# Fills and output pieces ahead of each step's turn in the second attention layer of a two-block transformer kernel

## The reference, cut to what matters

```
q, kc, vc, ks, vs, kw, vw, gl = split(h @ w_in)        # q: 1024 columns, each k and v: 256
q, ks, kw = rms_norm(q), rms_norm(ks), rms_norm(kw)    # over the 64 columns of a head
Kc = rms_norm(gelu(blocks(kc) @ w1) @ w2)              # 15 compressed keys
Vc = gelu(blocks(vc) @ w1) @ w2                        # 15 compressed values
p_c = softmax(q Kc^T * scale + bias)                   # 256 x 15 for each head
p_s = softmax(q ks^T * scale + bias)                   # 256 x 256, causal; every block is selected
p_w = softmax(q kw^T * scale + bias)                   # 256 x 256, causal
o = gate0 * p_c Vc + gate1 * p_s vs + gate2 * p_w vw
x = x + g1 * (o @ w_out)
```

## Time and profile before

| | before |
|---|---|
| median of 3 timed runs | 3153.59 us |
| lowest, highest | 3146.44, 3155.75 us |
| the profiled execution's own time | 3146.74 us |
| its span, first to last instruction | 3144.9 us |
| PE busy | 3072.9 us (98%) |
| DVE, ACT busy | 2251.2 us (72%), 1635.7 us (52%) |
| mean granted TensorE clock | 0.994 |
| the 48 steps of the loop | about 1093.8 to 1266 us of the span |

### The profile page before, as it was taken

The page is one execution under the profiler, slowest core; times in us unless marked ns, Lnnn a source line. Parts: engine busy times, 40 slices in busy tenths (PEclk is TensorE's granted clock), DMA queues, the critical chain, the costliest instruction groups (busy, mean ns, idle before and its releaser), DMA issues.

```text
span 3144.9 us, 58286 instructions
## 1 busy us (share of the span) xinstructions
PE 3072.9 (98%) x19860; PEld 2734.0 (87%) x19860; DVE 2251.2 (72%) x4124; ACT 1635.7 (52%) x3082; POOL 709.2 (23%) x710
## 2 busy tenths in 40 slices
PE   6999999999999999999999999999999999999999
PEld 5789999998788876799999888779988998988897
DVE  6649988877777535699788777777756777765654
ACT  1224568864444344355888544455456545445643
POOL 0106835530000010186555100000101010010000
PEclk9999999999999998999999999999999999999999
DMA  7644555558887441355444788877855687884454
GB/s 282 239 139 166 181 164 175 168 196 266 270 262 248 147 126 37 121 183 178 147 134 139 234 268 267 261 252 263 264 211 172 233 263 265 275 275 135 146 185 149
DMA packets 178353, 635.86 MB, mean 202 GB/s; under 512 B 24073, under 2 KB 24081, under 8 KB 177841
## 3 DMA queue, kind: packets, MB, share of 16 engines
q1 hardware_dynamic: 134560, 491.48, 47.4%
q0 software_dynamic: 43648, 142.77, 13.8%
q10 hardware_dynamic: 16, 0.01, 0.0%
HBM read 630.88 MB, written 9.53 MB: 204 GB/s over the span
## 4 chain that ended last, share of the span: by engine, by line
PE 85%; DVE 7%; DMA 3%; ACT 2%; DVEq 1%; issue 1%; SPq 0%; POOL 0%; ACTq 0%
PE ps L792 21%; PE ps L603 12%; PE ps L605 11%; PE ps L604 11%; PE ps L591 7%; PE ps L774 6%; PE ps L638 2%; PE ps L1190 2%; PE ps L1189 2%; DMA arena<-ada 1%; DMA ring<-stream 1%; PE ps L987 1%; PE ps L1054 1%; PE ps L892 1%; DVE r_outT L2459 1%
## 5 line engine op out<-in xcount | busy, mean ns | idle before, releaser
L1814 DVE TENSOR_TENSOR unit_low<-ring,unit_high 128x1024 fp32r<-128x1024 f32 x480 | 638.3, 1330 | 156.2 <-ACT unit_high L1297 147.3
L1297 ACT CAST unit_high<-ring 128x1024 fp32r<-128x1024 f32 x524 | 548.2, 1046 | 223.3 <-PE ps L605 165.4
L605 PE MATMUL ps<-expert_x_high,unit_low 128*128 128x256 f32 x1952 | 551.2, 282 | 0.0
L603 PE MATMUL ps<-expert_x_high,unit_high 128*128 128x256 f32 x1536 | 442.7, 288 | 2.5 <-DVE unit_low L1814 1.4
L604 PE MATMUL ps<-expert_x_low,unit_high 128*128 128x256 f32 x1536 | 428.4, 279 | 0.0
L605 PEld LDWEIGHTS ps<-expert_x_high,unit_low 128*128 128x128 f32 x1952 | 366.8, 188 | 0.0
L792 PE MATMUL ps<-unit_low,expert_high 128*128 128x512 f32 x1016 | 324.2, 400 | 1.3 <-DVE unit_low L1814 1.2
L792 PE MATMUL ps<-unit_high,expert_low 128*128 128x512 f32 x1016 | 319.5, 395 | 0.1
L792 PE MATMUL ps<-unit_high,expert_high 128*128 128x512 f32 x1016 | 316.6, 392 | 0.0
L603 PEld LDWEIGHTS ps<-expert_x_high,unit_high 128*128 128x128 f32 x1536 | 290.5, 189 | 7.3 <-issue 2.1
L1719 ACT CAST expert_high<-arena 128x256 fp32r (+1 forms) x256 | 103.7, 406 | 357.1 <-PE ps L792 357.1
(11 more groups left out here) (383 smaller groups left out, 7036.2 us busy)
## 6 DMA issues: line engine op xcount, KB each, us to landing
ring<-stream SPq DMA_DIRECT2D x754, 512.0 KB, 3.9
arena<-stream SPq DMA_DIRECT2D x160, 512.0 KB, 4.4
score<-ada POOLq DMA_DIRECT2D x128, 512.0 KB, 5.2
arena<-ada POOLq DMA_DIRECT2D x96, 512.0 KB, 5.3
arena<-bias_tiles POOLq DMA_DIRECT2D x48, 192.0 KB, 2.7
arena<-ada SPq DMA_DIRECT2D x8, 1024.0 KB, 17.3
bias_tiles<-bias_rows POOLq DMA_DIRECT2D x8, 768.0 KB, 14.9
arena<-gate_home POOLq DMA_DIRECT2D x7, 512.0 KB, 10.4
```

The lines of the kernel that those rows point to most:

```text
L603: pe.matmul(out, hi[:, kt, :], xh[:, kt, :], start=(kt == 0), stop=False)
L605: mm = pe.matmul(out, lo[:, kt, :], xh[:, kt, :], start=False, stop=(kt == KD - 1))
L1297: nc.scalar.copy(hi, raw_of(unit)).then_inc(whi_ready, 1)
L1814: V.tensor_tensor(out=lo, in0=raw_of(unit), in1=hi, op=ALU.subtract).then_inc(wlo_ready, 1)
```

## The change

In PE's loop, the fills and the output piece of a step now stand in front of the turn of that step and no longer behind it. The last pair of query chunks moves on: fill 26 goes from step 17 to 19, fill 27 from 18 to 20, fill 31 from 19 to 21. ACT reads the same table, so its copy and square after fill 27 and its root after fill 31 move by as many steps. DVE's two norms of that pair move from steps 20 and 21 to 22 and 23. The pieces swap their two PSUM banks: piece 0 goes to bank 0, which was free already, and the wait for the root after fill 31 (which reads bank 7) moves from piece 0 to piece 1. No instruction is added or taken away, and SP's and POOL's lists are the same.

```
-             11: (12, 15, 20), 12: (13, 21), 13: (22,), 14: (16, 23), 15: (24, 30), 16: (25,), 17: (26,), 18: (27,), 19: (31,)}
+             11: (12, 15, 20), 12: (13, 21), 13: (22,), 14: (16, 23), 15: (24, 30), 16: (25,), 19: (26,), 20: (27,), 21: (31,)}
...
                 for k in range(49):
-                    if k < 48:
-                        turn1(k)
                     for j in MIX1_FILL.get(k, ()):
                         fill(j)
                     if PIECE0 <= k < PIECE0 + 24:
                         j = k - PIECE0
-                        if j == 0:
+                        if j == 1:
                             pe.wait_ge(hn_std, hn + 12)
                         if j >= 2:
                             pe.wait_ge(y_taken, j - 1)
-                        piece(ps[0 if j % 2 else 7], j // 8, j % 8)
+                        piece(ps[7 if j % 2 else 0], j // 8, j % 8)
                         if j % 8 == 7:
                             pe.wait_ge(y_part, j + 1)
                             pe.sem_inc(unit_done, 2)
+                    if k < 48:
+                        turn1(k)
...
-                    if k in (16, 17, 20, 21):
-                        p, e = k // 20, k % 4 % 2
+                    if k in (16, 17, 22, 23):
+                        p, e = k // 20, k % 2
...
-                        add_piece(k - PIECE0, ps[0 if (k - PIECE0) % 2 else 7]).then_inc(y_taken, 1)
+                        add_piece(k - PIECE0, ps[7 if (k - PIECE0) % 2 else 0]).then_inc(y_taken, 1)
```

## The result

| | before | after |
|---|---|---|
| median of the timed runs (7 each) | 3151.16 us | 3167.38 us |
| lowest, highest | 3142.02, 3156.11 us | 3164.96, 3178.06 us |
| ratio after to before, 95% interval | | 1.0060, 1.0049 to 1.0072 |
| profiled execution's own time | 3146.74 us | 3167.38 us |
| its span | 3144.9 us | 3165.6 us |

The change makes the kernel slower by 0.6%; 3141 us and "faster" were forecast, and the time lies outside the range (3135 to 3156). The page's busy line of after answers to the earlier trace rows: PE is busy for 24 us more, with as many instructions.

The account below looks back on a forecast made before the run. PE was taken as the bound, busy 3072.9 of 3144.9 us. Gaps +2.9 and clock -9.5 gave -6.6 us against 3146.74, so 3140.1; with 1 us for handovers 3141 us, range 3135 to 3156.

Parts of the forecast that it names:

- Clock, -9.5: PE's half-clock stretch of 20.4 us from 1187.5 us goes and the clock stays high in the loop: -9.5 us.
- slow rival: Clock falls in the thin steps and stays down through the pieces, steps 17 to 31: about 3168 us; chance 9%.
- step 9: PE reaches fill 10 before ACT's gelu after fill 9 is done and waits: +1.5 us.
- Gap of step 0: The 2.55 us PE gap ahead of turn 0 is covered by fill 0; scores 3 then come late, +0.74 us.
- Every full step, +0.5: ACT's copy after a turn is just hidden behind the attend; small losses in short steps, together +0.5 us.
- The rival of the handover: ACT's copy is not hidden in each step, PE waits 0.19 us in 47 steps: 3149 us; chance 8%.
- Steps 13 and 16, +0.4 and +0.9: PE reaches scores 16 and scores 19 before ACT's copies are done: waits of +0.4 and +0.9 us.
- Step 21, +1.05: PE reaches fill 31 before ACT's square after fill 27 is done: +1.05 us.
- Step 22, +1.7: Scores 25 wait for ACT's copy behind root and table loads, the old 1.99 us gap moved: +1.7 us.
- End of the loop, +0.6: Turn 45 comes behind the last piece, so PE waits for ACT's last exponentials and normalize: +0.6 us.
- DVE in the thin steps, 0: DVE's norms in the thin steps make no turn wait in steps 17 to 25: taken as +0, at most 2 us.
- The gaps together, +2.9: New PE gaps of 7.4 us less old ones of 4.5 us: +2.9 us.

Follow-up runs that it names:

- e11: e2 with six dense matmuls of no use ahead of turn 19, where PE waits for DVE; median 3147.0 us, ratio to before 0.9988.
- e2: Kernel before with only the new table (last query pair two to three steps later), turn still in front; median 3145.5 us, ratio to before 0.9989.
- e4: After with only the pieces ahead of the turn, fills behind it; median 3151.0 us, ratio to before 1.0001.
- e13: After with fill 0 back behind turn 0; median 3173.6 us, ratio to before 1.0074.
- e15: Kernel before with only the fills of steps 1 to 12 ahead of their turns; median 3162.6 us, ratio to before 1.0043.
- e16: Kernel before with only the fills from step 13 on ahead of their turns; median 3149.4 us, ratio to before 1.0002.
- e12: Kernel before with eight dense matmuls of no use in the 1.99 us wait of step 20; median 3144.7 us, ratio to before 0.9985.
- e1: After's order (fills and pieces ahead of the turn) with the table of before; median 3168.8 us, ratio to before 1.0054.
- e3: After with only the fills ahead of the turn, pieces behind it; median 3162.8 us, ratio to before 1.0038.
- e10: After with 24 dense matmuls of no use in steps 4, 7 to 10, 17 and 18; median 3157.5 us, ratio to before 1.0019.
- e8: After with six dense matmuls of no use ahead of fill 10 in step 9; median 3162.6 us, ratio to before 1.0030.
- e5: After with the fill of step 9 back behind its turn; median 3164.1 us, ratio to before 1.0036.
- e6: After with the fills of steps 9, 13, 16 and 21 back behind their turns; median 3157.6 us, ratio to before 1.0026.
- e14: Kernel before with e12's eight dense matmuls in step 20 and fill 0 ahead of turn 0; median 3147.5 us, ratio to before 0.9999.
- e7: e2 with fill 0 ahead of turn 0, all other fills behind their turns; median 3149.6 us, ratio to before 0.9999.
- e9: After with the fills of steps 4 to 12 back behind their turns; median 3159.1 us, ratio to before 1.0028.

## Why the prediction was wrong, step by step

- **Clock, -9.5: the step that failed.** "I take it that it stays high" rested on the length of gaps: none left over 1.7 us, and one of 2.55 at full clock beside it. The clock lost 16 us more than in before instead of giving 9.5 back. With the gaps nearly right, this one term turned the sign. The gap beside it was a weak witness too, since it was read in one execution. At the same 2.55 us ahead of turn 0 the clock stayed at 1.00 in before and e11, and fell for 3.4 us in e2, e4, e13, e15 and e16. In e12, whose list is before's up to step 20, it was down for 10.2 us around the wait. That the order of the fills brings the loss is shown by e1, e3 and e15; that it is the clock and not work is shown by e10 and by the two sums.
- **Where I looked.** All rivals had the fall in steps 16 to 31. The second stretch came there as the slow rival said, and ended in step 25 as before, not in step 31. The first, from step 8 to step 11, stood in none. The change moved work there too, and I had priced only its wait (step 9, +1.5). Its fills are products of 30 columns between transposes and scores, not much wider than the products of 15 in front of the old fall, and I did not weigh them as such. That the slow rival's 3168 us meets the result is by chance: its mechanism is one of the two stretches.
- **Gap of step 0:** gone, and +0.57 at scores 3 (+0.74 forecast). Right.
- **Every full step, +0.5:** no gap opens, as said, but the size is low. At full clock turn follows turn in 3.04 us (1260.99 to 1264.03) against 3.00 in the earlier trace rows, and in 5.62 (steps 1 and 2) against 5.58 without a piece. At 0.04 us in some 40 steps that is 1.6 us. The rival of the handover had 0.19 a step and is false.
- **Step 9, +1.5:** 1.36 us in e1, e3, e13 and e15; hidden by the low clock in after. Mechanism right.
- **Steps 13 and 16, +0.4 and +0.9:** 0.29 and 0.69. **Step 21, +1.05:** 0.88 in e8 and e10, 0.89 in e5. Right within 0.3 us each.
- **Step 22, +1.7:** hidden by the low clock in after. In e2, with other cover in front, 0.81 is left, and in e6, with fill 31 behind turn 21, 0.26. Not measured at full clock in this order. In e1, where the table left the products in place, the old gap grew from 1.99 to 2.85.
- **End of the loop, +0.6:** 0.35.
- **DVE in the thin steps, 0:** holds for after, wrong for e2 (1.58 us ahead of turn 19, 1.01 ahead of turn 25), where the products stand behind the turn.
- **The gaps together, +2.9:** all work and waits came to +2 by the sum over runs, which is good to 1 or 2 us. The smaller terms are right as far as that can be told; the larger one is wrong.
- **Spread of before "may be this same stretch drawn out":** borne out in part. e12, without the stretch in its profile, has 11 runs of 3141.4 to 3149.6 against 33 of before beside it of 3140.8 to 3159.6.

## What to carry to other kernels

A stretch at the lower clock in the profile of before has to be costed as the largest term with both signs: here 20 us of it cost 7 to 10 us, and 44 us more of it cost some 20, against 4.5 us in the gaps that the change closed. When work is moved, look for thin work (few columns per matmul, short groups, a wait among them) in every stretch that the change touches, not only where the clock fell last time; PE's busy share does not show it. A mere change of order within such a stretch can bring the clock down, and dense matmuls that compute nothing, placed in a wait of PE, can pay (e12), though they do not make the clock safe (e14). One profile is one draw: the same list had the clock down in one execution and not in the next, so judge by the clocks of many runs.

## What the runs showed of the hardware that was not expected

- The clock fell to 0.50 with PE busy throughout: in after at 1135.5 the last gap in front was 0.57 us, 40 us earlier. In front of the fall were groups of matmuls of 30 columns, between turns and scores of 0.4 to 0.9 us.
- With PE busy at half clock (one wait of 0.21 us) it stayed down for 27.3 and 34.1 us in after. It rose the first time behind the first query product of 256 columns since the fall and a full turn (3.76 and 0.85 us, at 1157.10 and 1160.65), the second time in full turns beside pieces, and in e8 behind 6 dense products, after 13.7 us. That denser work brings it back is argued from this; in e14 eight dense products did not.
- A gap's length does not tell what it costs: 1.99 us among products of 15 columns went ahead of 20.5 us at half clock; 2.55 us ahead of turn 0, between full scores and a long product, went with full clock in before and with 3.4 us at half clock in e13, e15 and e16.
- The same program differs from run to run in how long the clock is down: e7 and e14 have two groups of runs, some 10 to 15 us apart in time.
- Open: what property of the order in steps 1 to 12 decides. A wait of 1.36 us among products of 30 columns went with the fall in all five runs of e15 (by their clocks), and in the profiles of e1, e3 and e13. But after and e9 fell without one in their profiles, e1, e8 and e9 fell for 6.8 us in step 4 as well, with no wait near, and e7 and e14 were slow in a third of their runs with the order of before in these steps. The wait is not the only cause; whether it makes the fall more certain was not tested by itself.
